# An attention stage rebuilt: heads in pairs, values stationary, probabilities divided before the transpose, mixer B first

## What is computed

```python
h = rmsnorm(x, norm_mix)
qa, ka, va, qb, kb, vb, ga, gb = split(h @ w_in + b_in)     # 16 q heads and 4 kv heads for A, 3 x 4 heads for B
ya = windowed_gqa(qa, ka, va, sinks, rel_bias)              # per head: softmax over keys and a sink logit
yb = dilated_attention(qb, kb, vb, rel_bias)                # 3 dilations (groups) of 4 heads, merged by softmax denominators
merged = sigmoid(ga) * (ya @ w_branch_a) + sigmoid(gb) * (yb @ w_branch_b)
x = x + merged @ w_out
x = x + moe(rmsnorm(x, norm_ffn))                           # top 4 of 32 experts, all 32 experts' weights are read
return rmsnorm(x, norm_final)
```

## Time and profile before

| | us |
|---|---|
| three runs, median (lowest to highest) | 1230.53 (1229.05 to 1230.85) |
| profiled execution, its own time | 1227.52 |
| its span in the trace | 1225.1 |
| PE busy, PE weight loads busy | 1142.7, 595.5 |
| DVE busy, ACT busy | 361.2, 236.1 |
| bytes moved by DMA | 448.38 MB |

### The profile page before, as it was taken

The page is one execution under the profiler, slowest core; times in us unless marked ns, Lnnn a source line. Parts: engine busy times, 40 slices in busy tenths (PEclk is TensorE's granted clock), DMA queues, the critical chain, the costliest instruction groups (busy, mean ns, idle before and its releaser), DMA issues.

```text
span 1225.1 us, 15428 instructions
## 1 busy us (share of the span) xinstructions
PE 1142.7 (93%) x6235; PEld 595.5 (49%) x6235; DVE 361.2 (29%) x767; ACT 236.1 (19%) x389; POOL 9.9 (1%) x18
## 2 busy tenths in 40 slices
PE   7999999999999999999989999898898989898996
PEld 6998998975434333433434333334243434343342
DVE  4446666543122212212122322121221212121212
ACT  5444456432110111101010110101000101010102
POOL 0000000000000000000000000000000000000000
PEclk9999999999999999999999999999999999999999
DMA  9956435567999999999999999999999999999992
GB/s 298 288 173 186 145 117 177 202 258 290 428 427 428 427 429 430 426 428 427 427 426 427 427 427 428 427 426 429 427 428 429 427 428 427 428 427 428 428 425 109
DMA packets 61139, 448.38 MB, mean 366 GB/s; under 512 B 4264, under 2 KB 32478, under 8 KB 36374
## 3 DMA queue, kind: packets, MB, share of 16 engines
q1 hardware_dynamic: 58778, 439.92, 87.0%
q0 software_dynamic: 1472, 5.51, 1.8%
q10 hardware_dynamic: 828, 2.02, 0.4%
HBM read 446.33 MB, written 1.11 MB: 365 GB/s over the span
## 4 chain that ended last, share of the span: by engine, by line
PE 64%; DMA 30%; DVE 2%; issue 1%; ACT 1%; SPq 0%; DVEq 0%; ACTq 0%
DMA slot<-in_w_up 30%; PE psum L1013 25%; PE psum L1050 8%; PE psum L953 5%; PE psum L701 5%; PE psum L703 5%; PE psum L702 5%; PE psum L771 2%; PE psum L968 1%; PE psum L976 1%; PE psum L1014 1%; PE psum L799 1%; PE psum L806 1%; PE psum L784 1%; DVE guT L1347 1%
## 5 line engine op out<-in xcount | busy, mean ns | idle before, releaser
L1013 PE MATMUL psum<-slot,xT 128*64 128x512 f32 x1024 | 450.0, 593 | 31.8 <-DMA slot<-in_w_up 29.6
L1014 PE MATMUL psum<-slot,xT 128*64 128x512 f32 x1024 | 450.5, 594 | 0.0
L1013 PEld LDWEIGHTS psum<-slot,xT 128*64 128x64 f32 x1024 | 137.4, 137 | 313.5 <-issue 298.7
L1050 PE MATMUL psum<-slot,guT 128*64 128x512 f32 x1024 | 237.2, 605 | 26.4 <-ACT xT L655 26.4
L1341 DVE COPY gu<-psum 128x512 f32<-128x512 f32 x32 | 33.4, 1043 | 567.1 <-PE psum L1014 567.1
L1050 PEld LDWEIGHTS psum<-slot,guT 128*64 128x64 f32 x1024 | 73.6, 138 | 164.3 <-issue 154.4
L1014 PEld LDWEIGHTS psum<-slot,xT 128*64 128x64 f32 x1024 | 137.4, 137 | 0.3
L671 ACT COPY gu<-psum 128x512 f32<-128x512 f32 x32 | 34.1, 1066 | 407.9 <-PE psum L1014 407.9
L1104 DVE TENSOR_TENSOR pieces<-raw,pieces 128x2048 fp32r<-128x2048 f32 x32 | 73.3, 2292 | 72.1 <-ACT pieces L506 72.1
L701 PE MATMUL psum<-hT_hi,pieces 128*128 128x256 f32 x296 | 84.7, 286 | 0.0
L702 PE MATMUL psum<-hT_lo,pieces 128*128 128x256 f32 x296 | 83.7, 283 | 0.0
(11 more groups left out here) (178 smaller groups left out, 935.9 us busy)
## 6 DMA issues: line engine op xcount, KB each, us to landing
slot<-in_w_gate SPq DMA_DIRECT2D x64, 2048.0 KB, 34.8
slot<-in_w_up SPq DMA_DIRECT2D x64, 2048.0 KB, 37.1
slot<-in_w_down SPq DMA_DIRECT2D x63, 2048.0 KB, 35.9
raw<-in_w_in SPq DMA_DIRECT2D x23, 1024.0 KB, 5.8
raw<-in_w_branch_a SPq DMA_DIRECT2D x4, 1024.0 KB, 5.3
raw<-in_w_out SPq DMA_DIRECT2D x4, 1024.0 KB, 4.9
windows<-bias_table POOLq DMA_DIRECT2D x8, 384.0 KB, 4.5
windows<-bias_table POOLq DMA_DIRECT2D x4, 576.0 KB, 7.1
```

Source lines behind the costliest of these rows:

```text
L1013: mm(bank(GU + nb)[0:CAP, :], x_k, gate[:, c, cols], start=k == 0, stop=k == KC - 1)
L1014: done = mm(bank(GU + nb)[CAP:P, :], x_k, up[:, c, cols], start=k == 0, stop=k == KC - 1)
L1050: done = mm(bank(DOWN)[half * CAP:(half + 1) * CAP, :], hidden[:, k, :], down[:, c, half * BANK:(half + 1) * BANK], start=k == 0, stop=k = ...
```

## The change

- **Order of the pieces.** q, k and v of mixer B come first (0 to 8), then k, v and q of A (9, 10, 11 to 14), then gates. A table `ORDER` maps a piece to its columns in `w_in`.
- **Units.** 14 pairs of heads `w`: six of mixer B (dilation `w % 3`, heads 0 and 1, then 2 and 3) and eight of mixer A. The two heads of a pair always lie in the two row halves of the array (partitions 0 to 63, 64 to 127).
- **Logits.** The factor of the scores goes into the copies of the queries and their biases. One DVE instruction (`tensor_tensor_reduce`, L1163) adds the window to 256 logits and takes the row minimum of their negative; four for a pair, in place of one add for each head and one maximum for a group.
- **Division first.** `normalise` (L1200) multiplies the probabilities by a ratio on DVE before the transposes: four instructions of 128 x 256 for a pair. For mixer B the ratios of three pairs are made together, in four small steps; for A in two.
- **Weighing.** In `weigh` (L840) the 64 columns of values are the stationary operand and the 256 columns of transposed probabilities stream, heads 0 and 1 of a pair to the two column halves (PSUM partitions 0 to 63, 64 to 127). The result comes out transposed, as the branches need it: `turn_mix`, `divide`, `yb`, the reload of x and their semaphores are gone. ACT and DVE split it from PSUM (`mix_hi`, `mix_lo`, 128 x 256 each, ten of each).
- **Order.** PE makes the logits of pair w after piece 6 + w, its transposes after piece 10 + w and its weighing after piece 11 + w. Branch B's eight output blocks go by twos (`branch_b(k)`), with the last transposes and weighings between; the bias transposes stand behind piece 24 (m = 0 of branch A).
- **Buffers.** `probs` has four places of a pair, the bias windows two places of a pair (14 loads for 12). `load_tenth(2)` waits for the last weighing, now just ahead of branch A.

```diff
-            for n in range(GROUPS):
-                if n + 2 < GROUPS:
-                    scores(n + 2, FIRST)
-                if n < N_GATE:
-                    project(GATE_A + n)
-                if n + 2 < GROUPS:
-                    scores(n + 2, REST)
-                turn(n)
-                if n >= 1:
-                    weigh(n - 1)
+            for p in range(1, W_B):
                 project(p)
+                slot_no = p - FIRST_SLOT
+                if 0 <= slot_no + 3 < N_PAIRS:
+                    scores(slot_no + 3)
+                if 0 <= slot_no - 1:
+                    turn(slot_no - 1)
+                if 0 <= slot_no - 2:
+                    weigh(slot_no - 2)
...
+                for jt in range(TT):
+                    for i in range(2):
...
+                        last = mm(mix_bank(j)[i * DH:(i + 1) * DH, :], values, probsT[:, w % 2, i, jt, :],
+                                  start=first and jt == 0, stop=final and jt == TT - 1)
+                last.then_inc(weighed, 1)
...
+            branch_b(0)
+            branch_b(1)
+            turn(N_PAIRS - 1)
+            weigh(N_PAIRS - 2)
+            branch_b(2)
+            branch_b(3)
+            weigh(N_PAIRS - 1)
...
+            def logits_of(w):
...
+                        last = v.tensor_tensor_reduce(
+                            probs[:, w % PROBS, i, iq, :], bank(SCORE[i])[:, iq * S:(iq + 1) * S], window(w, i, iq), -1.0,
+                            floor, ALU.add, ALU.min, minus_peak[:, w, c:c + 1])
...
+                for i in range(2):
+                    for iq in range(2):
+                        c = 2 * i + iq
+                        p = probs[:, w % PROBS, i, iq, :]
+                        last = v.tensor_scalar(p, p, ratio[:, w, c:c + 1], None, ALU.mult)
+                last.then_inc(norm_done, 1)
```

More of the change, by code:

```diff
@@ new lines, in exps @@
+            def exps(w):
+                act.wait_ge(logits_done, w + 1)
+                for i in range(2):
+                    for iq in range(2):
+                        c = 2 * i + iq
+                        v = probs[:, w % PROBS, i, iq, :]
+                        last = nc.scalar.activation(v, v, ACT.Exp, bias=minus_peak[:, w, c:c + 1], scale=-1.0,
+                                                    accum_out=den[:, w, c:c + 1])
+                if w < B_PAIRS and w % NG == NG - 1:
+                    v = more[:, w - NG + 1:w + 1, :]
+                    last = nc.scalar.activation(v, v, ACT.Exp)
+                elif w >= B_PAIRS:
+                    v = more[:, w, :]
+                    last = nc.scalar.activation(v, v, ACT.Exp)
+                last.then_inc(exps_done, 1)
@@ L871, in _ @@
                     last.then_inc(gu_bias_up, 1)
[L872 to L890 removed]
+            pe.wait_ge(gu_bias_done, 1)
             for tt in range(TT):
@@ L1110, in _ @@
                     dve.wait_ge(columns_up, 1)
-                    v.tensor_copy(columns[:, :], bank(COLUMNS)[:, 0:int(T_END) + KC]).then_inc(columns_done, 1)
+                    for t0, t1, scale in ((T_QA, T_KA, SCALE), (T_KA, T_QB, 1.0), (T_QB, T_KB, SCALE), (T_KB, T_END + KC, 1.0)):
+                        r = slice(int(t0), int(t1))
+                        last = v.tensor_scalar(columns[:, r], bank(COLUMNS)[:, r], scale, None, ALU.mult)
+                    last.then_inc(columns_done, 1)
                 inverse_rms(tt, 1, tt + 1)
@@ L1128, in copy_gates @@
                 last.then_inc(gate_copied, 1)
-            def logits_of(n, some):
-                kind, heads = groups[n]
-                if n >= 3:
-                    dve.wait_ge(turned_up, first_unit[n - 2])
-                dve.wait_ge(window_in[n % 2], 16 * (n // 2 + 1))
-                for i in range(len(heads))[some]:
-                    u = first_unit[n] + i
-                    dve.wait_ge(scores_up, u + 1)
-                    last = v.scalar_tensor_tensor(probs[:, n % 3, i, :, :], bank(SCORE[u % 2]).rearrange(
-                        "p (a b) -> p a b", a=2), SCALE, window(n, i), ALU.mult, ALU.add)
-                    last.then_inc(logits_done, 1)
```

542 lines of the change are left out of this document (254 added, 288 removed).

## The result

| | before | after |
|---|---|---|
| four runs side by side, median (lowest to highest), us | 1229.79 (1227.47 to 1230.85) | 1208.01 (1206.04 to 1210.80) |
| ratio of the times, 95% interval | | 0.9823 (0.9809 to 0.9838) |
| profiled execution, its span | 1227.52, 1225.1 | 1210.80, 1208.2 |
| PE, PE weight loads, DVE, ACT busy | 1142.7, 595.5, 361.2, 236.1 | 1135.4, 575.6, 359.5, 241.9 |
| mean granted clock of PE | 0.991 | 0.986 |

The median fell by 21.8 us, and the prediction had 1208. Between the two profiled executions the span fell by 16.9 only. So the sum has to be read term by term, since one number that fits does not say that its terms do.

What follows compares the result with a forecast made beforehand. MoE weight streaming fixes the end behind the first expert's start, and PE's chain sets the first stage. -25.7 + 3.1 = -22.6 us takes 1227.5 to 1204.9; the median, 3.0 higher, is 1208, range 1202 to 1218.

Steps and rivals of the forecast that it cites:

- What bounds the kernel: MoE weight streaming: the end stands a fixed distance behind the first expert's start, so first-stage savings pass on one to one.
- The stretch up to branch A, -25.7: From piece 6's end to branch A: 169.3 us becomes 143.6, 25.7 less.
- if PE never waits: Condition on the 143.6 us stretch to branch A: PE's own work alone fills it.
- the Trainium skill's rival: Mode changes drain the engine: each of 14 weighings pays a second 0.2, 2.8 us, giving 1211; chance 0.07.
- Of the 25.7: Split of the saving: weighing 9.4, mixer B logits about 4.5, turning back 2.2, bias transposes 2.0, waits some 7.6.
- Step of 8.95: PE's attention step: logits 1.07, transposes 0.87, weighing 1.07, piece with mode change 5.94 us.
- DVE: DVE's step 7.4 us, fused instruction 0.55, no PE wait; DVE bound between 0.94 and 1.34 had chance 0.07.
- Branch A, +3.1: Branch A 26.0 us for 23.0: bias transposes 2.0, waits 0.7, 0.2 and rounding; 3.1 more.
- Ring, cost nothing: Fourth weight load 10.7 us ahead of w_out's end, 4 us dry time remaining, no cost; late-ring rival 0.02.
- The cover: Pieces beside attention steps: some 7.6 us of gain put to waits, including the last four groups without a piece.
- Copy before the last weighing 1.6 us from being late: Tail rival, with DVE in branch A already late: 3 to 8 us, 1211 to 1216; chance 0.08.
- the sum of 22.6: Whole first stage: -25.7 + 3.1 = -22.6 us, from 1227.5 to 1204.9 for the profiled execution.

Runs made afterwards that it cites:

- the experiment: Changed kernel with both heads of each mixer B pair taking logits from one row half: ratio to before 0.9854 (0.982 to 0.9887), median 1209.03 us.
- three and nine more: Changed kernel with three, or nine, more 128 x 256 DVE instructions in each dividing step: ratios to before 0.9822 and 0.9865.
- The late ring: Changed kernel with the ring's fourth weight load held until x is ready for the MoE: ratio to before 0.989 (0.9862 to 0.9917).

## Why the prediction was right, point by point

- **What bounds the kernel.** Right. The distance from the eleventh load to the end is the same 922.5, and every us before it passed on.
- **The stretch up to branch A, -25.7.** It is -25.4. With PE's own rows the sum is 97.9 for pieces and branch B, 14 x 1.06 of logits, ten transposes at 1.02 and four at 0.87, 14 x 1.01 of weighing and 19 x 0.18 of changes: 144.0, where the trace has 143.9. So PE waits for nothing, the "if PE never waits" of the text. Weighing came 0.06 a pair under the 1.07 (0.9 in all), and the Trainium skill's rival (one more change a weighing, 1211) did not come at the weighings. A part of its 2.8 us came at the transposes instead, as the step of 9.04 below shows.
- **Of the 25.7.** Weighing was given 9.4 and is 24.4 - 14.1 = 10.3. Logits were given "about 4.5", and stay there: the 5.1 of the experiment is for six pairs in one half, while in the kernel before one group of eight in mixer B already took 1.07. The waits were what was left over, 7.6. Of the 25.4 the named terms now leave 6.4, and 7.9 with the 1.5 that the transposes became dearer. But 1.0 of that is the group of logits at low clock in the kernel before (2.08 for 1.07), which was counted as a wait: chance in the profile that the prediction was built on. No experiment on the kernel before measured the waits by themselves.
- **Step of 8.95.** It is 9.04. The term that was mis-sized is the transposes, 0.87 in the sum for a row that stood behind a piece, and 1.02 where the order puts them behind the logits. The price of a change of mode was taken for the way back to fast matmuls alone. It costs 1.3 to 1.5 us in all, and weighing's 0.9 happened to pay for most of it.
- **DVE.** The forecast of no wait was right. Its fused instruction was put at 0.55 and is 0.41 (bounds 0.40 and 0.86); a step is 6.9 and not 7.4. The slack, 1.6 us a step by the prediction, is 2.1; three and nine more bound it from both sides.
- **Branch A, +3.1.** Without the low clock it is 25.84 where it was 23.0, +2.8: 2.0 of transposes and 0.2 for the change of mode, as said, and 0.5 of waits for the 0.7 of the sum. In the profile it is +3.9, since a low clock, which the sum did not have, costs 1.5 and hides the 0.5.
- **Ring, cost nothing.** Right. The fourth load is 11.9 ahead of x ready (252.15 - 240.22), predicted 10.7, and a dry time remained. In a profile without low clock it is 2.2 us, not 4, so the ring is nearer to its limit than I said. The late ring shows what lies past it.
- **The cover.** "Copy before the last weighing 1.6 us from being late" was no issue, but the worth of a piece beside a step, had it gone, was not priced: 2.4 us a step and, with four such steps, a clock that costs as much again.
- **What the agreement of the numbers hides.** The profile is 1210.8, the sum for it 1204.9. The 5.9 between them are the start (1.3; it lies between 57.4 and 59.5 over the profiles), the stretch (0.3), branch A (0.8, by 1.0 of clock), the way to the MoE (3.2, all of it clock: 33.5 for 28.6 at full clock, where the kernel before had 30.3, with 1.7 of clock in it), and 0.3 of rounding and of what lies around the span. The median of four is 21.8 under the old one, which is 0.8 less than the sum of 22.6. A profile shows one execution with its stretches of low clock; a median of four or five is good to some 2 to 4 us, as the intervals say. So the 1208.0 is right within that, and the exact hit is chance.

## What to carry to other kernels

Where small matmuls fill only half of the array's rows or columns, put two side by side in different halves: eight of them cost 1.9 us in one half and 1.0 in two. Keep independent work beside each step of a dependent chain, since an uncovered step costs the whole round trip over ACT and DVE (2.4 us here), and here the clock fell behind such waits too. Before a profile's difference is given to the change, compare the granted clock of the stretches that were not changed.

## What the runs showed of the hardware that I had not expected

- A transpose group of eight behind row-half matmuls is 0.15 us longer than behind full-array ones (1.02 for 0.87). Put behind a piece instead, it lost that again, and the stretch 1.26 us over ten groups.
- The fused add-and-minimum of 128 x 256 from PSUM keeps the pace of a plain instruction of that shape (0.41), and the read of its accumulator is free behind it.
- PE's granted clock fell in a stretch in which PE was busy all the time: 4.00 of 4.00 us at 208 to 212 and 0.65 at 212 to 216, the same instructions at 1.00 in other executions. It cost 1.5 us there, as matmuls 0.12 apart went to 0.21. It fell also where PE had waited: to 0.50, the 1.2 GHz level, from 192 to 208 with four steps uncovered (0.58 busy of 4.00 just before), and to 0.57 at 202 to 206 with nine more instructions on DVE (1.66 busy of 4.00 just before). The first kind moves this program by some 1 to 6 us from one execution to the next, more than several of the edits that were tried. What brings it on stays open.
